# Keys transposed by the crossbar in steps 9 to 23, weight conversions in half packets, one tile's norm sums on VectorE

## The reference

```
q, f_logit, i, o_gate, glu_v, glu_g, gate_a, gate_b = split(x @ w_in)
A:  f = lb + (1-lb)*sigmoid(f_logit);  k = 1-f;  g = log f;  q = silu(q)/sqrt(128)
    S_t = diag(f_t) S_(t-1) + k_t v_t^T,  o_t = S_t^T q_t        (8 heads, 128x128 state)
    y_a = (rms_norm(o) * silu(o_gate)) @ w_hg_out
B:  u = depthwise causal conv, 31 taps, of glu_v*sigmoid(glu_g)
    y_b = silu(layer_norm(u)) @ w_conv_out
h = layer_norm(alpha*x + (sigmoid(gate_a)*y_a + sigmoid(gate_b)*y_b) @ w_out)
out = layer_norm(alpha*h + (silu(g)*u) @ w_ffn_out),  [g, u] = h @ w_ffn_in   (2816 hidden)
```

## Time and profile before

| | |
|---|---|
| time, median of 3 runs | 2329.2 us (2324.72 to 2329.82) |
| the profiled execution, its own time | 2328.88 us |
| its span (core 7, the slowest) | 2326.9 us |
| spans of the eight cores | 2319.0 to 2326.9 us |
| TensorE busy | 2276.8 us, 98% |
| VectorE, ScalarE, POOL busy | 1122.9, 961.2, 427.0 us |
| data moved | 431.84 MB |

### The profile page before, as it was taken

How to read it: one execution, slowest core, us unless ns; L and a number is a source line. 1 busy time by engine, 2 the same in 40 slices (tenths; PEclk the granted TensorE clock), 3 DMA queues, 4 the chain that set the end, 5 groups by cost and what they waited for, 6 DMA issues and landing times.

```text
span 2326.9 us, 39871 instructions; the slowest of 8 cores (2319.0 to 2326.9 us)
## 1 busy us (share of the span) xinstructions
PE 2276.8 (98%) x14164; PEld 1128.7 (49%) x14164; DVE 1122.9 (48%) x1829; ACT 961.2 (41%) x1267; POOL 427.0 (18%) x526
## 2 busy tenths in 40 slices
PE   7999999999998999999999999999999999999997
PEld 3555555555555554544444444444444444444543
DVE  4566555565557677335345344443533623621522
ACT  3677777777776674231331230241232223211110
POOL 0111111111110011122320320311411410300212
PEclk9999999999999999999999999999999999999999
DMA  7766997897888569899965764864864773764551
GB/s 230 110 111 129 151 148 139 139 162 140 150 167 201 173 226 295 254 202 224 280 217 150 255 217 143 254 205 158 242 197 157 245 219 139 204 208 146 161 205 68
DMA packets 151442, 431.84 MB, mean 186 GB/s; under 512 B 43584, under 2 KB 76352, under 8 KB 122048
## 3 DMA queue, kind: packets, MB, share of 16 engines
q1 hardware_dynamic: 135664, 379.12, 54.7%
q0 software_dynamic: 15584, 50.17, 15.8%
HBM read 421.22 MB, written 70.05 MB: 211 GB/s over the span
## 4 chain that ended last, share of the span: by engine, by line
PE 90%; DMA 4%; ACT 2%; issue 2%; DVE 2%; SPq 1%; POOL 0%; DVEq 0%; POOLq 0%; ACTq 0%
PE pst L488 89%; DMA sb_cpre<-ys 1%; DMA sb_stg<-xt 1%; DMA sb_W<-w 1%; SPq L574 1%; ACT L515 1%; DMA ys<-sb_y 1%; PE pst L500 1%; ACT sb_F L515 0%; DMA sb_W<-w2b 0%; DVE sb_U L533 0%; DVE sb_q L533 0%; DVE sb_q L524 0%; DVE sb_F L857 0%; ACT sb_rs L515 0%
## 5 line engine op out<-in xcount | busy, mean ns | idle before, releaser
L488 PE MATMUL pst<-sb_hT,sb_W 128*128 128x512 bf16 (+1 forms) x2880 | 610.2, 374 | 0.0
L488 PE MATMUL pst<-sb_xT,sb_W 128*128 128x512 bf16 x2560 | 591.5, 379 | 9.2 <-DVE sb_v L541 3.6
L488 PEld LDWEIGHTS pst<-sb_hT,sb_W 128*128 128x128 bf16 x2880 | 281.8, 98 | 326.1
L515 ACT ACTIVATE sb_q<-pst 128x512 f32<-128x512 f32 x296 | 176.0, 595 | 600.1 <-PE pst L488 589.7
L488 PEld LDWEIGHTS pst<-sb_xT,sb_W 128*128 128x128 bf16 x2560 | 246.0, 98 | 302.6 <-issue 17.0
L488 PE MATMUL pst<-sb_W,sb_xT 128*128 128x256 bf16 (+1 forms) x2048 | 357.6, 327 | 13.1 <-ACT sb_xT L557 6.6
L488 PE MATMUL pst<-sb_W,sb_actb 128*128 128x512 bf16 x1408 | 308.3, 380 | 3.6 <-DVE sb_actb L524 2.3
L524 DVE TENSOR_TENSOR sb_actb<-sb_q,pst 128x512 bf16<-128x512 f32 x176 | 120.6, 687 | 363.8 <-PE pst L488 354.2
L488 PEld LDWEIGHTS pst<-sb_W,sb_xT 128*128 128x128 bf16 x2048 | 196.5, 98 | 137.6 <-issue 21.2
L488 PEld LDWEIGHTS pst<-sb_W,sb_actb 128*128 128x128 bf16 x1408 | 138.0, 98 | 171.5 <-issue 6.9
L533 DVE SCALAR_TENSOR_TENSOR sb_q<-sb_q,pst 128x512 f32<-128x512 f32 x120 | 82.2, 687 | 242.2 <-PE pst L488 210.3
(11 more groups left out here) (106 smaller groups left out, 2013.0 us busy)
## 6 DMA issues: line engine op xcount, KB each, us to landing
sb_W<-w2b SPq DMA_DIRECT2D x202, 1024.0 KB, 7.7
sb_T<-tabb SPq DMA_DIRECT2D x64, 632.0 KB, 7.8
w2b<-w POOLq DMA_DIRECT2D x38, 512.0 KB, 10.5
ys<-sb_y SPq DMA_DIRECT2D x64, 256.0 KB, 8.9
sb_cpre<-ys SPq DMA_DIRECT2D x32, 512.0 KB, 7.7
sb_R<-x SPq DMA_DIRECT2D x8, 2048.0 KB, 11.4
out<-sb_R SPq DMA_DIRECT2D x31, 512.0 KB, 9.4
sb_W<-w2b SPq DMA_DIRECT2D x14, 768.0 KB, 5.3
```

Of the source, the lines that this page charges most:

```text
L488: i = e.matmul(o, lhsT=l, rhs=r, start=s0, stop=s1)
L515: P.add("act", lambda e: e.activation(out=out, in_=in_, func=func, **kw), ks(in_, scale, bias) + list(er), (ks(out) if wkeys is None else ...
```

## The change

- In steps 9 to 23 (XA to XB−1) the keys go from K3 to `ktm` by one DMA transpose on SP's queue, in place of 8 transposes on TensorE and a copy. In the other steps TensorE transposes as before.
- K3 is laid out anew: what is transposed is one run of 1024 columns; the second chunks of each 128 lie 1088 columns further on. A memset fills 1024 columns once.
- `v` has two buffers; `osq` takes the memory of `Am`. In steps 9 to 23 the projection of v stands ahead of the output products.
- The conversions of phase 1 are cut so that each DMA takes two runs of 1024 columns of a row in place of one of 2048.
- T loads are written into the program two units ahead throughout.
- In `conv_ln(2)` the 14 additions are VectorE's.
- DMA_SHARE, a number of the planner's model, becomes 0.5 for both queues.

```diff
-DMA_SHARE = {"sp": 0.37, "pool": 0.63}
+DMA_SHARE = {"sp": 0.5, "pool": 0.5}
+XB = 24
+XA = 9
...
-        K3 = A.at("K3", take(4096), [128, 2, 8, 2, 64], BF16)
+        K3 = A.at("K3", take(4352), [128, 2176], BF16)
-        vt = A.at("v", take(2048), [128, 4, 256], BF16)
+        vt = [A.at(f"v{i}", take(2048), [128, 4, 256], BF16) for i in range(2)]
-        osq = A.at("osq", take(2048), [128, 2, TS], BF16)
+        osq = A.at("osq", pos[0] - 2048, [128, 2, TS], BF16)
...
+        def dma_t(out, in_, sem):
+            if sem not in dsems:
+                dsems[sem] = es.enter_context(nc.semaphore("d_" + sem))
+            P.add("sp", lambda e: e.dma_start_transpose(out=out, in_=in_), ks(in_), ks(out), dsem=sem, dur=0.45, nb=1.6)
+        memset(K3[:, 1024:2048], 0.0)
...
-            if g + 2 < CG:
-                conv_load(q, g + 2)
+            if G + 2 < 4 * CG:
+                conv_load(*divmod(G + 2, CG))
...
-                pT = newps("h")
-                pv = pT[:, 0:512].bitcast(BF16)
-                Kf = [K3[:, h].rearrange("p c s t -> p (c s t)") for h in range(2)]
-                trg([(pv[:, (h * 4 + b) * 128:(h * 4 + b + 1) * 128], Kf[h][:, b * 256:b * 256 + 128])
-                     for h in range(2) for b in range(4)], identB[:])
-                cp_any(ktm[:].rearrange("p h a b -> p (h a b)"), pv)
-                relps("h", pT)
+                if XA <= s < XB:
+                    dma_t(ktm[:].rearrange("p h a b -> p (h a) b"), K3[:, 0:1024], "kt")
+                else:
+                    pT = newps("h")
+                    pv = pT[:, 0:512].bitcast(BF16)
+                    trg([(pv[:, k * 128:(k + 1) * 128], K3[:, k * 128:(k + 1) * 128]) for k in range(8)], identB[:])
+                    cp_any(ktm[:].rearrange("p h a b -> p (h a b)"), pv)
+                    relps("h", pT)
...
+            for f in ((upd, vproj, outp) if XA <= s < XB else (upd, outp, vproj)):
+                if live if f == vproj else s >= 1:
+                    f()
+                    yield
...
+            Kb = K3[:].rearrange("p (o x) -> p o x", o=2)
+            for o in (1, 0):
+                c2 = lambda a: flat(a).rearrange("p (c o t) -> p o c t", o=2, t=64)[:, o]
+                Ko = Kb[:, o, 0:1024].rearrange("p (c s t) -> p c s t", s=2, t=64)
+                stt(Ko[:, :, 0, :], c2(F1[:]), 1.0, c2(F2[:]), ALU.subtract, ALU.mult)
+                if o:
+                    Ka = Kb[:, 0, 0:1024].rearrange("p (c s t) -> p c s t", s=2, t=64)
+                    for h in range(2):
+                        tt_(Ka[:, 4 * h:4 * h + 4, 1, :], Ko[:, 4 * h:4 * h + 4, 0, :],
+                            E[:, h, 1:9:2].unsqueeze(2).broadcast_to([128, 4, 64]), ALU.mult)
...
         def cast(b, k, gate):
-            dma("pool", w2b_d[b, :, k * 2048:(k + 1) * 2048], w2_d[b, :, k * 2048:(k + 1) * 2048], f"cw{group(b)[0]}",
+            part_ = lambda a: a.rearrange("p (q c) -> p q c", q=2)[:, :, k * 1024:(k + 1) * 1024]
+            dma("pool", part_(w2b_d[b]), part_(w2_d[b]), f"cw{group(b)[0]}",
...
-                        tt_(S1[:], cpre[:, 0, :] if j == 1 else S1[:], cpre[:, j, :], ALU.add, eng="pool")
-                        tt_(S2[:], prev[:] if j == 1 else S2[:], sq[:], ALU.add, eng="pool")
+                        tt_(S1[:], cpre[:, 0, :] if j == 1 else S1[:], cpre[:, j, :], ALU.add, eng="dve" if i == 2 else "pool")
+                        tt_(S2[:], prev[:] if j == 1 else S2[:], sq[:], ALU.add, eng="dve" if i == 2 else "pool")
```

More of the change, by code:

```diff
@@ L722, in conv_unit @@
             relps("c", ps)
-            if g + 2 < CG:
-                conv_load(q, g + 2)
+            if G + 2 < 4 * CG:
+                conv_load(*divmod(G + 2, CG))
         def c_thread():
             for q in range(5):
-                if q > 0:
-                    conv_load(q - 1, 0)
-                    conv_load(q - 1, 1)
+                if q == 1:
+                    conv_load(0, 0)
+                    conv_load(0, 1)
                 for k in range(NBLK if q < 4 else CG):
@@ L762, in pair @@
                 pp_, tp = divmod(s - 1, NST)
-                vp, ogp, rp = vt, og[(s - 1) % 2], rb[(s - 1) % 2]
+                vp, ogp, rp = vt[(s - 1) % 2], og[(s - 1) % 2], rb[(s - 1) % 2]
             def proj(W, c0):
@@ L788, in pair @@
             if s >= 1:
-                pT = newps("h")
-                pv = pT[:, 0:512].bitcast(BF16)
-                Kf = [K3[:, h].rearrange("p c s t -> p (c s t)") for h in range(2)]
-                trg([(pv[:, (h * 4 + b) * 128:(h * 4 + b + 1) * 128], Kf[h][:, b * 256:b * 256 + 128])
-                     for h in range(2) for b in range(4)], identB[:])
-                cp_any(ktm[:].rearrange("p h a b -> p (h a b)"), pv)
-                relps("h", pT)
+                if XA <= s < XB:
[6 more added lines that the diff above has]
+                    relps("h", pT)
                 pA = newps("h")
                 mmg([(pA[:, h * 512 + b * 128 + hf * 64:h * 512 + b * 128 + hf * 64 + 64],
-                      Kf[h][:, b * 256 + hf * 64:b * 256 + hf * 64 + 128],
+                      K3[:, hf * 1024 + (h * 4 + b) * 128:hf * 1024 + (h * 4 + b) * 128 + 128],
                       Qp[:, h, b * 128 + hf * 64:b * 128 + hf * 64 + 64], True, True)
@@ L815, in pair, with upd @@
                 yield
-            if s >= 1:
+            def upd():
                 pK = newps("h")
@@ L825, in pair, with vproj, outp @@
                 relps("h", pK)
-                yield
-            if s >= 1:
+            def vproj():
+                v = vt[s % 2]
+                ps = newps("h")
+                for tb in range(4):
+                    mmg([(ps[:, tb * 256:(tb + 1) * 256], xT[:, t, kc, tb * 128:(tb + 1) * 128], Woi[:, kc, 256:512],
+                          kc == 0, kc == 7) for kc in range(8)])
+                cp_any(v[:].rearrange("p a b -> p (a b)"), ps)
+                relps("h", ps)
+            def outp():
                 pO = newps("h")
@@ L843, in pair @@
                 return
[L844 to L851, removed]
             for h in range(2):
@@ L1084, in h_trans @@
                 cp(b[:], R[:, tb, :], eng="act")
[L1085 to L1090, removed]
+                dma_t(hT[:, :, tb * 128:(tb + 1) * 128], b[:], f"ht{tb}")
                 yield
```

1 line of the change is left out of this document (removed).

## The result

The changed kernel takes 2353.22 us (median of 4 runs, 2347.08 to 2414.88) against 2329.51 for the kernel before: ratio 1.0099, 95% interval 1.0085 to 1.0113, so about 23 us slower. The prediction was 2320.5 us, range 2315 to 2327.5, and gave "slower" a chance of 0.08. One chip of the experiments ran the cores 4 to 7 of every kernel at a lower clock, and executions with one disturbed half of the chip are left out of all ratios.

A forecast was written before the change was run, and what follows sets the result against it. TensorE, busy 98% of the span, was taken to bound the kernel; 2328.9 − 6.9 (key transposes) − 1.4 (tile 2's sums) = 2320.6, all other parts 0, predicted as 2320.5 us, range 2315 to 2327.5.

The forecast's parts named there:

- Landings of 8.6 to 10.7 us, 3 us left even of the smallest slack. Cost 0: Steps 9 to 23: crossbar keys land before the product with v reads ktm, slack 14.0 to 17.6 us, so no cost.
- the late rival: Steps 9 to 23: crossbar keys land behind conversions and T loads, TensorE waits each step, 32 us, 2352.6 in all; chance 0.08.
- My turning point: Steps 9 to 23: mean key lateness of 0.87 us a step, above which the kernel is slower by more than 0.2%.
- Conversions in halves: 0: Phase 1 conversions on POOL's queue: twice the packets, same bytes; gain bounded by a 0.8 us wait for T, taken as 0.
- The planner's shares: within ±3 us, in the holes of 660 to 900: DMA_SHARE 0.5/0.5 reorders all engines; only TensorE's 16.7 us of holes there can move, 3 us either way, taken as 0.
- −6.9 us on TensorE: Steps 9 to 23: 15 groups of 8 key transposes leave TensorE, 0.46 us each, all on the path.
- Tile 2's sums: −1.4: Near 1045 us: sums moved from POOL to VectorE free VectorE and then TensorE 1.4 us earlier.
- The SP queue: T loads behind a transpose wait 1.4 us for the queue; 13 us of cover remain, else TensorE waits 0.8 us.
- Given back at the end of phase 1: From 660 to 900 a new order adds 3 us of holes and tile 2 loses 1: 2326.0; chance 0.17.
- More than planned: Tile 2's hole goes whole (2.3 us) and holes of 660 to 900 shrink by 3: 2316.7; chance 0.09.
- The slower rival: The same as the late rival: keys too late in steps 9 to 23, 2352.6 us; chance 0.08.
- the three signs of "wrong": Over 5 us of waits for ktm, holes from 660 to 900 above 20 us, or several new holes around 1040.

The follow-up runs named there:

- b2: The kernel before with the conversions in halves alone; ratio 0.9989 to the kernel before.
- e1: The changed kernel with the old DMA_SHARE of 0.37/0.63; ratio 1.0073 to the kernel before.
- f1: The changed kernel with whole-length conversions and the old DMA_SHARE 0.37/0.63, crossbar kept; ratio 1.0000 to the kernel before.
- e2: The changed kernel with conversions in whole packets, new shares kept; ratio 1.006 to the kernel before.
- g5: The changed kernel with old shares, conversions in quarters and all keys transposed on TensorE; ratio 1.0002 to the kernel before.
- g4: The changed kernel with old shares and conversions in quarters, crossbar kept, second run of it; ratio 0.9975 to the kernel before.
- g3: A repeat of e1 (changed kernel, old shares, conversions in halves); ratio 1.0073 to the kernel before.
- f3: e1 with the projection of v moved ahead of the product with ktm in steps 9 to 23; ratio 1.0072 to the kernel before.
- g1: The changed kernel with its own new shares and conversions in quarters in place of halves; ratio 1.0010 to the kernel before.
- f7: The changed kernel with old shares and conversions in quarters, crossbar kept, first run of it; ratio 0.9979 to the kernel before.

## Why the prediction was wrong, point by point

- **"Landings of 8.6 to 10.7 us, 3 us left even of the smallest slack. Cost 0": the step that failed first.** The landings' median was nearly right (10.7 on core 3, 11.0 over all cores), and so was the slack (14.1 to 14.4 in the tight steps). But I set a median against a slack where the tail decides: the longest landings were 20.0 us on core 3 and 21.6 over all. My own worst row was 17.9, and I used it for a rival in which every transfer is that late. One late transfer in five or six (one in three in the tight steps) was enough, since a us of waiting costs 1.3 with the clock behind it, and eight cores draw from that tail while the slowest counts. The tail has an address: 15 of the 22 late keys met two or three outstanding conversions, the very case that the prediction names as that of the late rival without counting how often it occurs. My turning point, a mean lateness of 0.87 us a step, is 13 us a core. The mean here was 77 / 8 = 9.6, and it was slower all the same, by the clock and by the spread.
- **"Conversions in halves: 0": wrong twice.** Halves alone did cost nothing (b2) and bring 3.4 us at the end of the span, for which the sum had no term. But with the crossbar they made 22 to 26 keys late in place of 4 to 14. I priced the edit by itself, beside an engine that nothing waited for, and not against the new transfer. From the rule of the Trainium skill that I cited, "DMA: Bandwidth & Descriptors", section "Queues, rings and completion order", that each engine takes its queues in turn packet by packet, I had drawn that the keys land the same with halves or whole packets. The runs don't bear out what I drew: halves were worse in time than whole packets (e1 against f1, the changed kernel against e2), and quarters better than halves.
- **"The planner's shares: within ±3 us, in the holes of 660 to 900": wrong place, wrong size.** They cost 8 to 13 us at 1030 to 1060, by one swap in GpSimd's order: a weight load behind additions that wait for transfers. I looked for the price where there were holes before; a reordering makes its hole where a load had just enough lead. The row that warned is in the earlier trace rows: GpSimd stood there for each landing of cpre.
- **"−6.9 us on TensorE": right for half of the steps.** I take the time from one product with ktm to the next (medians of eight cores) and add it up over the 15 steps with crossbar: 401.4 us before, 402.7 in g5, 397.7 in g4. So the crossbar with its order of groups brings 5.0. The rest of the change that g5 keeps (layout, buffers, place of the T loads) costs 1.3 that I had set at 0: −3.7 in place of −6.9. From before to g4, eight of the 15 fall by 3.1 us together, 0.39 each (26.31 to 25.87 at most), but the other seven by 0.6 (27.0 to 27.5 in both). In those, it seems, short waits take the place of the transposes; one of them, on core 3 of g4:

```profile
449.66 0.53 PE L490 MATMUL pst<-sb_T,sb_u 128*32 128x128 bf16 x32 [0.42 <-DVE sb_u L535]
```
- **"Tile 2's sums: −1.4": misread.** The row of 1045 is tile 3's. No run shows a gain above what the measurement can tell.
- **The SP queue.** I held its cover against the T loads, and they were fine (waits of 0 to 2.2 us a core). I didn't ask what the queue does to the transpose itself: most late keys (15 of 22) are among the 24 of 120 whose issue took over 2.5 us. Whether the long issue makes a key late, or both come from a full DMA, no run separates.
- **"Given back at the end of phase 1", "More than planned": neither.** The slower rival named the right place and gave 2352.6 us, against 2353.22 measured, but by another sum, so the nearness is luck: 32 us of late keys, where core 3, the slowest, lost 17.9 in the key stretch and 5.9 in the weight stretch (208.3 against 202.4) and won 3.4 at the end. Its chance of 0.08 was too low because it asked for every key to be late. Of the three signs of "wrong" the first came, over 5 us of waits for ktm (17.2 on core 3). In place of several new holes around 1040 there came one for W near 1060, of 3.3 to 10.6 us on every core. The holes from 660 to 900 stayed just under 20 us (19.6 on core 3). A slip in the last line of the sum, 2320.5 where 2320.6 and 0.3 make 2320.9, changes nothing.

What stays open: why halves are worse than both whole packets and quarters. The key stretch is also 6 to 7 us longer with the old shares (e1 against the changed kernel, f1 against e2), although every engine has the same order up to 1000 us. Most of that is more waiting for keys: 13.5 us a core against 9.6, and 6.1 against 1.3, which at 1.29 makes 5.0 of 5.9 and 6.2 of 7.4 us. Each of these is one profile, so the count of late keys for one and the same order can lie at 4 (e2) or at 14 (f1); that the shares themselves make keys late is not shown.

## What to carry to other kernels

Set the tail of a transfer's landings, not their median, against the slack of its reader, and multiply by the cores when the slowest sets the time: what most cores win, one loses. Look for what the tail goes with, such as the bulk transfers outstanding at the issue, and count how often the program brings that about; moving the conversions away from the tight steps was not tried here. A number in a scheduler's cost model is an edit to every queue. Compare the order of each engine before and after, and look for a load that has come to stand behind instructions that wait for other transfers. Try the grain of bulk transfers next to a latency-bound one in more than one step, since the effect need not go one way. And cut the span to its very end before a gain is put down to the part that was meant to bring it.

## What the runs showed of the hardware that was not expected

- A crossbar transpose of 256 KB lands at 2.7 us at best and, beside conversions in halves, at 21.6 to 27.1 at worst (changed, e1, g3, f3); beside quarters at 14.7 to 16.5 (g1, g4, f7). Its issue holds SyncE's queue for 1.2 us or up to 15.5 (f3).
- The grain of the conversions (POOL's queue) has no monotone effect on it, with the old shares: whole, halves, quarters, eighths gave 14, 24 to 26, 2 to 3 and 6 late keys of 120 (with the new shares 4, 22 and 3). At 364 bytes a packet conversions landed after 25.3 us, transposes after 20.0, and the kernel lost 5%.
- A hole on TensorE costs more than itself: the clock granted was 0.76 over the 10 us after the hole of 5.80 at 334 (2.4 us more), and 0.90 over the 70 us around core 7's hole of 10.57 us (0.98 from 1040 to 1110 before). Over 64 cores a us of waiting for keys made the key stretch 1.29 us longer.
- GpSimd's closing DRAIN is longer the fewer and longer the packets of its conversions were: 9.57, 6.22, 5.32 and 3.77 us with whole, halves, quarters and eighths, the same to 0.01 us on every core. It ends the span of the first two.
